# Gating and squares of a state-space scan by chunk of tokens, one SiLU earlier, rotation angles one group later

## The reference, cut to what matters

```python
xbc = jax.nn.silu(conv(xbc) + conv_b)            # 4 taps, per channel; x, B, C are split from it
y = ssd_chunked(xs, dt, a, bm, cm)               # scan over 4 chunks of 128 tokens
y = y + d_skip[:, None] * xs
y = y.reshape(b, s, D_INNER) * jax.nn.silu(z)    # gating
yg = y.reshape(b, s, SSM_GROUPS, D_INNER // SSM_GROUPS)
yg = yg * lax.rsqrt(jnp.mean(yg * yg, axis=-1, keepdims=True) + EPS)
y = yg.reshape(b, s, D_INNER) * gnorm_w
return y @ out_w
```

## Time and profile before

| | |
|---|---|
| median of 3 runs | 1403.54 us |
| the profiled execution | 1402.74 us, of which the span is 1400.9 us |
| PE busy | 1364.5 us (97%) |
| DVE, ACT, GpSimd busy | 824.8 us (59%), 683.6 us (49%), 529.2 us (38%) |
| granted TensorE clock | 0.993 over the span, 1.00 in every stretch from 0 to 900 us |

### The profile page before, as it was taken

The page is one execution under the profiler, slowest core; times in us unless marked ns, Lnnn a source line. Parts: engine busy times, 40 slices in busy tenths (PEclk is TensorE's granted clock), DMA queues, the critical chain, the costliest instruction groups (busy, mean ns, idle before and its releaser), DMA issues.

```text
span 1400.9 us, 17933 instructions
## 1 busy us (share of the span) xinstructions
PE 1364.5 (97%) x6664; PEld 1075.1 (77%) x6664; DVE 824.8 (59%) x1435; ACT 683.6 (49%) x1146; POOL 529.2 (38%) x259
## 2 busy tenths in 40 slices
PE   8999999999999999999999999999999999999998
PEld 6877777777778878767888887766677788888887
DVE  5576464757567744785677323467745654544665
ACT  6654635636366443684555312344645423232563
POOL 3553554635320034466000344134452655555200
PEclk9999999999999999999999999989999999999999
DMA  5222222212232232211333342130013233333331
GB/s 189 91 75 61 90 62 83 84 61 75 75 92 91 90 91 91 61 46 53 99 90 122 104 135 76 51 101 16 16 31 91 91 96 100 92 104 91 111 100 61
DMA packets 33078, 116.81 MB, mean 83 GB/s; under 512 B 3932, under 2 KB 4316, under 8 KB 32736
## 3 DMA queue, kind: packets, MB, share of 16 engines
q1 hardware_dynamic: 31976, 111.85, 25.8%
q10 hardware_dynamic: 1016, 3.81, 0.8%
HBM read 113.55 MB, written 2.10 MB: 83 GB/s over the span
## 4 chain that ended last, share of the span: by engine, by line
PE 88%; DVE 4%; ACT 3%; issue 2%; POOL 1%; DMA 1%; ACTq 0%; DVEq 0%
PE bank L1289 85%; PE bank L1744 1%; PE bank L1587 1%; ACT wsh L850 1%; DMA h<-in_xT 1%; POOL arena L760 0%; PE bank L1463 0%; POOL wsl L702 0%; DVE arena L1985 0%; ACT arena L1225 0%; PE bank L1498 0%; DVE arena L2271 0%; DVE arena L1905 0%; DVE arena L2185 0%; PE bank L1742 0%
## 5 line engine op out<-in xcount | busy, mean ns | idle before, releaser
L702 POOL TENSOR_TENSOR wsl<-ring,wsh 128x1024 fp32r<-128x1024 f32 x144 | 351.6, 2442 | 565.1 <-ACT wsh L850 565.0
L850 ACT ACTIVATE wsh<-ring 128x1024 fp32r<-128x1024 f32 x199 | 210.6, 1058 | 460.6 <-PE bank L1289 437.5
L1289 PE MATMUL bank<-parts1h,wsh 128*128 128x512 f32 (+1 forms) x736 | 293.5, 399 | 10.3 <-POOL wsl L702 3.4
L1289 PE MATMUL bank<-parts1h,wsl 128*128 128x512 f32 (+1 forms) x736 | 286.5, 389 | 0.0
L1289 PE MATMUL bank<-parts1l,wsh 128*128 128x512 f32 (+1 forms) x736 | 286.4, 389 | 0.0
L1289 PE MATMUL bank<-parts0h,wsh 128*128 128x512 f32 x704 | 281.2, 399 | 3.6 <-issue 1.3
L1289 PE MATMUL bank<-parts0h,wsl 128*128 128x512 f32 x704 | 274.5, 390 | 0.0
L1289 PE MATMUL bank<-parts0l,wsh 128*128 128x512 f32 x704 | 274.2, 390 | 0.0
L1289 PEld LDWEIGHTS bank<-parts1h,wsh 128*128 128x128 f32 x736 | 139.0, 189 | 47.9 <-issue 7.1
L1289 PEld LDWEIGHTS bank<-parts0h,wsh 128*128 128x128 f32 x704 | 132.1, 188 | 40.5 <-issue 8.6
L1289 PEld LDWEIGHTS bank<-parts1h,wsl 128*128 128x128 f32 x736 | 139.0, 189 | 29.2
(11 more groups left out here) (319 smaller groups left out, 1806.7 us busy)
## 6 DMA issues: line engine op xcount, KB each, us to landing
ring<-in_wstream SPq DMA_DIRECT2D x206, 512.0 KB, 3.6
arena<-in_alibi ACTq DMA_DIRECT2D x2, 1024.0 KB, 5.2
outT<-arena SPq DMA_DIRECT2D x8, 256.0 KB, 2.6
h<-in_xT SPq DMA_DIRECT2D x2, 256.0 KB, 5.7
h<-in_xT ACTq DMA_DIRECT2D x2, 256.0 KB, 6.4
h<-in_xT SPq DMA_DIRECT2D x1, 512.0 KB, 8.3
h<-in_xT ACTq DMA_DIRECT2D x1, 512.0 KB, 9.2
arena<-in_cmpb ACTq DMA_DIRECT2D x1, 496.0 KB
```

The costliest lines, as they stand in the source:

```text
L702: return nc.gpsimd.tensor_tensor(dst, src, hi.bitcast(F32), ALU.subtract)
L850: nc.scalar.activation(wsh[n % NSET][:, :], src, ACT.Copy).then_inc(*done("high", ("high", L)))
L1289: return nc.tensor.matmul(*args, **kw)
```

## The change

It does four things. (1) The gating, squaring and summing go by chunk of tokens instead of by 128 channels: a step `yc(g, c)` multiplies, squares and sums the 4x128 values of chunk c; the sum over the four channel tiles is one `tensor_reduce` that reads with m innermost, 128 elements (512 B) apart. The steps for c = 0, 1, 2 stand right behind ssd2(g,3), that for c = 3 behind ssd3(g,3). (2) In group 3, gn(3) stands behind sout(2,5) instead of sout(2,6). (3) The SiLU of proj(0,5) is issued in ssd0(0). (4) `angles` moves behind ssd1(1,0), `sines` behind ssd1(1,3).

```diff
@@ -149,19 +149,24 @@
         else:
             nxt, so = proj[3], sout[2]
             fill = nxt[7:8] + so[:2] + nxt[8:9] + so[2:4] + nxt[9:] + [("psp", 0)] + so[4:5]
-            head, mid, tail = so[5:7], so[7:] + [("pp", 0, 0)], [("pp", 0, m) for m in (1, 2, 3)]
+            head, mid, tail = so[5:6], so[6:] + [("pp", 0, 0)], [("pp", 0, m) for m in (1, 2, 3)]
         k = 0
         for i, x in enumerate(scan):
             out.append(x)
-            if x == ("ssd0", 0):
+            if x == ("ssd2", g, 3):
+                out += [("yc", g, c) for c in range(3)]
+            if x == ("ssd3", g, 3):
+                out.append(("yc", g, 3))
+            if x == ("ssd1", 1, 0):
                 out.append(("angles",))
-            if x == ("ssd1", 0, 3):
+            if x == ("ssd1", 1, 3):
                 out.append(("sines",))
             while k < len(fill) and k * len(scan) < (i + 1) * len(fill):
                 out.append(fill[k])
                 k += 1
         out += fill[k:]
-        out += [("yt", g, m) for m in range(GT)] + head[:1] + [("ya", g)] + head[1:] + [("gn", g)] + mid + [("gb", g)] + tail
+        out += [("ya", g)] + head + [("gn", g)] + mid + [("gb", g)] + tail if g == 3 else \
+            head[:1] + [("ya", g)] + head[1:] + [("gn", g)] + mid + [("gb", g)] + tail
     def early(name, m):
         return [("he", name, m)]
 
@@ -569,7 +574,7 @@
         yoef = ar(36, SEQ)
         ysq = ar(37, SEQ)
         yac = ar(38, SEQ)
-        ysq2 = ar(36, SEQ)
+        ysqb = [ysq, sq[:, 1, :]]
         dtb = ar(39, NT, HEADS)
         da = ar(39.25, NT, HEADS)
         dtmp = ar(39.5, NT, HEADS)
@@ -948,7 +953,7 @@
                     else:
                         silu_open()
                         if g >= 1:
-                            act.wait_ge(*at("ygated", g - 1, i - 6))
+                            act.wait_ge(*at("ygated", g - 1, NT - 1))
                         nc.scalar.activation(zs[:, i - 6, :], b[:, :], ACT.Silu)\
                             .then_inc(*done("zs", ("zs", g, i - 6), ("free", *step)))
                 if k == "dtl":
@@ -973,6 +978,8 @@
                     act.wait_ge(*at("mm", "lg"))
                     nc.scalar.activation(acT, ps(("lg",))[:, :], ACT.Copy).then_inc(*done("acT_high", ("acT_high",)))
                 if k == "ssd0":
+                    if a[0] == 0:
+                        silu_open()
                     act.wait_ge(*at("mm", "bt", *a))
                     if a[0] >= 1:
                         act.wait_ge(*at("mm", "st", a[0] - 1, 2))
@@ -1004,13 +1011,14 @@
                         act.wait_ge(*at("mm", "yo", g - 1, 3))
                     nc.scalar.activation(prev[1], ps(("st", g, 0))[:, :].rearrange("p (a b) -> p a b", a=HPG), ACT.Copy)\
                         .then_inc(*done("prev1", ("prev", g, 1), ("free", "st", g, 0)))
-                if k == "yt":
-                    g, m = a
-                    act.wait_ge(*at("ygated", g, m))
-                    if m == 3:
-                        act.wait_ge(*at("yadd", g, 1))
-                    nc.scalar.activation([yac, ysq, ysq2, ysq][m], xs[g % 2][:, m, :], ACT.Square)\
-                        .then_inc(*done("ysq", ("ysq", g, m)))
+                if k == "yc":
+                    g, c = a
+                    n = g * NT + c
+                    act.wait_ge(*at("ygated", g, c))
+                    if n >= 2:
+                        act.wait_ge(*at("yadd", (n - 2) // NT, (n - 2) % NT))
+                    nc.scalar.activation(ysqb[c % 2].rearrange("p (m t) -> p m t", m=GT), xs[g % 2][:, :, tok(c)], ACT.Square)\
+                        .then_inc(*done("ysq", ("ysq", g, c)))
                 if k == "gn":
                     g = a[0]
                     link(nc.scalar.activation(tiny[:, :], eps[:, :], ACT.Ln))
@@ -1998,21 +2006,23 @@
                     dve.wait_ge(*at("mm", "yot", g, c))
                     nc.vector.tensor_tensor(x, x, ps(("yot", g, c))[:, :].rearrange("p (a b) -> p a b", a=GT), ALU.add)\
                         .then_inc(*done("ysum", ("ysum", g, c), ("free", "yot", g, c)))
-                if k == "yt":
-                    g, m = a
-                    dve.wait_ge(*at("ysum", g, NT - 1))
-                    dve.wait_ge(*at("zs", g, m))
-                    nc.vector.tensor_tensor(xs[g % 2][:, m, :], xs[g % 2][:, m, :], zs[:, m, :], ALU.mult)\
-                        .then_inc(*done("ygated", ("ygated", g, m)))
-
-                def yadd(g, m):
-
-                    dve.wait_ge(*at("ysq", g, m))
-                    if m >= 2:
-                        dve.wait_ge(*at("yadd", g, m - 1))
-                    nc.vector.tensor_tensor(yac, yac, ysq2 if m == 2 else ysq, ALU.add).then_inc(*done("yadd", ("yadd", g, m)))
-
-                if k == "yt" and a[1] >= 2:
+                if k == "yc":
+                    g, c = a
+                    x = xs[g % 2][:, :, tok(c)]
+                    dve.wait_ge(*(at("ysum", g, c) if c else at("yskip", g, 0)))
+                    for m in range(GT if c == 0 else 0):
+                        dve.wait_ge(*at("zs", g, m))
+                    nc.vector.tensor_tensor(x, x, zs[:, :, tok(c)], ALU.mult).then_inc(*done("ygated", ("ygated", g, c)))
+
+                def yadd(g, c):
+
+                    dve.wait_ge(*at("ysq", g, c))
+                    if g and c == 0:
+                        dve.wait_ge(*at("mm", "gn", g - 1))
+                    nc.vector.tensor_reduce(yac[:, tok(c)], ysqb[c % 2].rearrange("p (m t) -> p t m", m=GT), AXX, ALU.add)\
+                        .then_inc(*done("yadd", ("yadd", g, c)))
+
+                if k == "yc" and a[1] >= 1:
                     yadd(a[0], a[1] - 1)
                 if k == "ya":
                     yadd(a[0], 3)
```

## The result

The changed kernel takes 1412.25 us (median of 4 runs, 1410.1 to 1412.55), the kernel before, run beside it, 1403.63 us (4 runs, 1401.39 to 1404.27): a ratio of 1.0062, 95% interval 1.0048 to 1.0075. It is slower, by 8.6 us, where 6.0 us (1409.1 us) had been forecast. Its profiled execution took 1410.1 us with a span of 1408.3 us, 7.4 us above that of before, at the same mean granted clock (0.992 and 0.993). The other three runs had spans of 1410.2 to 1410.7 us.

What follows compares the result with a forecast made beforehand. PE, busy 97% of the span, was taken as the bound. Terms -0.44 + 2.51 + 4.19 + 0.23 - 0.50 = +5.99 us gave 1409.1 us, with 8 in 10 between 1405.0 and 1412.5.

Steps and rivals of the forecast that it cites:

- The first SiLU: Start of group 0: PE's 2.48 us wait goes, but a convolution is late next, so only -0.44 us.
- The angles: Group 1: the chain goes ahead of hadd on a DVE without gaps and moves PE by its length, +2.51 us.
- The ends of groups 0 to 2: Early chunk squares hold ACT's next weight copy: +0.23 us in group 1, nothing in groups 0 and 2.
- the copies behind gn: Groups 0 and 2: a PE wait, from four squares in a row holding the weight copy, goes; 0.25 us each, -0.50 us.
- The reduce: DVE's strided sum of 512 values was taken as 1.05 us, bounds 0.68 (stride free) and 1.4 us.
- The end of group 3: Last sum 1.47 us later, and sout(2,6)'s 2.72 us of matmuls come after gn(3)'s wait: +4.19 us.
- the angles find room: Rival, chance 0.12: other waits cover the angles in group 1, the +2.51 us goes: 1406.6, or 1405.1 with free strides.
- the sum is early: Rival, chance 0.05: reduce 3 over by 383.5, gn(3) does not wait, -1.25 instead of +4.19 us: 1403.7 us.
- DVE's work is absorbed: Rival, chance 0.06: gates, reduces and angles run in DVE's idle time; 4.2 us are saved: 1398.9 us.
- the SiLU gives just the 0.44: Rival without a stated chance: the SiLU at the start is not earlier, which would cost just the 0.44 us.
- The one that gave 1412 us: Rival, chance 0.12: GpSimd holds the gates, next copies late by up to 1 us in three groups, reduce slower: +9 us.

Runs made afterwards that it cites:

- e2_angles_g0: The changed kernel with angles and sines back in group 0: 1407.64 us (6 runs), ratio 1.0033 to the kernel before.
- e7_angles_later: The changed kernel with angles moved to behind ssd3(1,1) and sines to behind ssd3(1,2), later in group 1: 1407.27 us in one run.
- e8_warm: The changed kernel with 24 unused matmuls added on PE between sout(2,5) and gn(3): 1412.03 us in one run.
- e6_gn_bank: The changed kernel with gn(3)'s inverse root written to SBUF, so its bank is free behind the Ln: 1413.9 us in one run.
- e1_gn_late: The changed kernel with gn(3) back behind sout(2,6): 1405.07 us (11 runs), ratio 1.0019 to the kernel before.
- e11_gn_early_only: The kernel before with only gn(3) moved to behind sout(2,5): 1409.75 us in one run.
- e10_best_shift: The changed kernel with gn(3) behind sout(2,6), angles and sines in group 0, contiguous reduce, group 0's fill one scan step earlier: 1409.31 us (5 runs), ratio 1.0042.

## Why the prediction was right, and where it fell short

The direction and the mechanisms hold, and the time, 1412.25 us, is inside the range, but at its upper end. Step by step, against the stretches:

- **The first SiLU**: -0.44 forecast, -0.32 measured. The wait of about 2 us for the convolution is where it was said to be.
- **The angles**: +2.51 forecast, +2.49 measured; the two waits, 1.9 and 0.5 us (forecast 2 and 0.7), stand where they should. `e2_angles_g0` and `e7_angles_later` show that the place is the cause. What the step left out is what a wait of 2 us can bring behind it: where the clock fell there, the price was 3.3 us (*g1* 57.4).
- **The ends of groups 0 to 2**: +0.23 forecast for group 1, +0.32 measured. Taking off the 1.20 us by which group 1's last `yskip` is late in all (219.66 and 220.86), the copies start at 224.32 and 230.27 and POOL ends at 233.79, within 0.03 us of the chain as it was worked out. For the copies behind gn, -0.50 forecast; -0.34 each in groups 0 and 2 and -0.08 in group 1, -0.76 in all.
- **The reduce**: 1.05 us taken from the add with a stride of 64 B, 1.07 us measured at 512 B. The rule of the Trainium skill, page "SBUF — State Buffer", section "Door 1: The DMA port swizzle", under which each new 16-byte line has its price, agrees with this number, and with the 1.13 us of ACT's square when it writes in steps of 16 B. The Trainium skill's page "VectorE: DVE Perf Modes", section "Mode 1× (REGULAR) — the baseline", would have given the plain 0.68 us, and does not agree.
- **The end of group 3**: this is the term that was mis-sized. The sum was +4.19; 1.41 + 5.28 = +6.69 was measured. Its two parts were right, 1.41 for 1.47 (taking off the 1.13 us by which `yskip` is late, gn(3) starts at 389.02 instead of the 389.07 of the chain) and 2.72 for the matmuls. Missing were two terms that the sum put at nothing. After 5.4 us of idleness PE came back at half clock (1.44 us, `e8_warm`). And I asked only whether sout(3,0) waits for y behind gn. But the job that inherits gn(3)'s bank, the sixth behind it, is now pp(0,3) and no longer sout(3,0), and the scaling that frees the bank comes later: on DVE it stands behind the `hadd` of sout(2,7), and there are now two quarters of sout between gn(3) and that `hadd`, not one. It starts 8.6 us behind gn(3) (398.77 and 390.15), where before it did so after 4.5 us (below, and 387.60). That costs 0.99 us (`e6_gn_bank`).

DVE in the kernel before, behind gn(3); the scaling is over at 396.29, ahead of sout(3,0) at 396.72:

```profile
391.48 0.69 DVE L2036 TENSOR_TENSOR h<-h,bank 128x512 f32<-128x512 f32 x1 [3.43 <-PE bank L1289]
392.09 2.06 DVE L2024 SCALAR_TENSOR_TENSOR arena<-arena,vec,bank 128x512 f32<-128x512 f32 x3
...
395.56 0.73 DVE L2024 SCALAR_TENSOR_TENSOR arena<-arena,vec,bank 128x512 f32<-128x512 f32 x1
```

The scan's sum is +8.48 instead of +5.99, and the two missing terms, clock and bank, make 2.43 of the 2.49. The median's +8.6 is 1.2 us above that of the profiled span; the other three runs were 1.9 to 2.4 us longer than the profiled one. Those runs have no trace, so where they lost it stays open: half clock in group 1 or at the start, 0.8 and 1.6 us in the experiments, would give as much, but their mean granted clock (0.992 or 0.993) is no lower than that of the profiled one. The same 2 us show in the medians of `e1_gn_late` and `e2_angles_g0`, which are 7.2 and 4.6 us below 1412.25 where their stretches *gn3* and *g1* give 5.28 and 2.49.

So the 8.6 us are 2.6 more than the forecast's 6.0: 2.5 more in the scan, 1.1 less in what lies ahead of it and behind it, and the 1.2 by which the runs lie above the profiled one.

The rivals: that the angles find room fell with *g1*; that the sum is early, or that DVE's work is absorbed, fell with the 5.4 us at gn(3). That the SiLU gives just the 0.44 is the forecast's own term. The one that gave 1412 us came near the time but for no reason of its own: its gates would have been held by GpSimd, and they took 0.60 us from start to start (382.19 and 382.79), as forecast without it. A number that fits is no support for the case that named it.

## What to carry to other kernels

A step that waits must not be moved ahead of work that covered its wait unless somebody behind it needs the result: the price is the work passed over, and to it come the bank that the step holds and the clock that an idle TensorE may lose. A small chain on a shared engine is free where that engine idles next and costs its full length where a wait of the bounding engine ends behind it; read the queue from there to the next gap (2.5 us at 175 us, nothing at 198 us). Before a layout is turned to spare one engine a stride, look who writes it: the stride moved from DVE's 1.07 us to ACT's 1.13 us, and ACT had the next weight copy behind it. Before an operand is moved from PSUM to SBUF to free a bank, look whether GpSimd is in flight there: the scaling went from 0.74 to 2.89 us.

## What the runs showed of the hardware that I had not expected

- The granted clock fell to half within some 2 us of the end of waits of 2.0 and 2.5 us (start; `e11_gn_early_only` for the latter), 1.9 us (`hadd`), 2.4, 4.0 and 5.4 us (gn(3)) and 2.6 and 2.8 us (`yot`, `e10_best_shift`), and in other executions did not at the same 2.0 us, nor behind one of 2.7 us at gn(3).
- DVE's scaling of 512 values took 0.74 us with one tensor in a PSUM bank while GpSimd's L707 was in flight, 0.74 us with both in SBUF while it was not, and 2.89 us with both in SBUF while it was. The 2.15 us more lie inside the 2.41 us of L707 (`e6_gn_bank`).
- DVE's reduce over four values 512 B apart takes 1.07 us for 512 values, contiguous 0.68 us; ACT's square with an output in steps of 16 B 1.13 us instead of 0.63 us.
